# Down projections of a decoder layer on TensorE: column blocks in pairs, four of eleven inner blocks by seven products instead of eight

## The reference

```python
def swiglu(x, w_gate, w_up, w_down):
    return (jax.nn.silu(x @ w_gate) * (x @ w_up)) @ w_down
...
h = x
f = swiglu(rmsnorm(h, g_ffn1_pre[i]), w_ffn1_gate[i], w_ffn1_up[i], w_ffn1_down[i])
h = h + 0.5 * rmsnorm(f, g_ffn1_post[i])
u = rmsnorm(h, g_mix_pre[i])
...
h = h + rmsnorm(o, g_mix_post[i])
f = swiglu(rmsnorm(h, g_ffn2_pre[i]), w_ffn2_gate[i], w_ffn2_up[i], w_ffn2_down[i])
h = h + 0.5 * rmsnorm(f, g_ffn2_post[i])
```

## Time and profile before

| | |
|---|---|
| three runs | 1891.41, 1890.99, 1890.77 us; median 1890.99 |
| span of the profiled execution | 1889.1 us |
| what lies around the span, by the median | 1.9 us |
| PE, DVE, ACT, POOL busy in the span | 1878.1, 1080.5, 883.9, 112.8 us |
| matmuls | 8658 |
| DMA | 371.54 MB, mean 197 GB/s |

### The profile page before, as it was taken

How to read it: one execution, slowest core, us unless ns; L and a number is a source line. 1 busy time by engine, 2 the same in 40 slices (tenths; PEclk the granted TensorE clock), 3 DMA queues, 4 the chain that set the end, 5 groups by cost and what they waited for, 6 DMA issues and landing times.

```text
span 1889.1 us, 24728 instructions
## 1 busy us (share of the span) xinstructions
PE 1878.1 (99%) x8658; PEld 1550.4 (82%) x8658; DVE 1080.5 (57%) x1208; ACT 883.9 (47%) x1179; POOL 112.8 (6%) x162
## 2 busy tenths in 40 slices
PE   9999999999999999999999999999999999999998
PEld 7888888888888888888888888888888888888886
DVE  5555555455544446777896755555555454444565
ACT  6444444444444346555555644444444344344563
POOL 1000000000000001013551100000000000000010
PEclk9999999999999999999999999999999999999999
DMA  7666666666665655655556566666666666656554
GB/s 258 202 207 202 203 193 193 210 214 215 204 202 196 200 195 165 201 168 167 152 178 204 165 212 207 203 203 207 202 193 193 202 229 198 201 192 207 191 190 145
DMA packets 214115, 371.54 MB, mean 197 GB/s; under 512 B 16592, under 2 KB 41632, under 8 KB 213664
## 3 DMA queue, kind: packets, MB, share of 16 engines
q1 hardware_dynamic: 213040, 367.20, 61.5%
q10 hardware_dynamic: 1008, 3.46, 0.5%
HBM read 358.01 MB, written 2.10 MB: 191 GB/s over the span
## 4 chain that ended last, share of the span: by engine, by line
PE 98%; DVE 1%; ACT 0%; issue 0%; POOL 0%; POOLq 0%; DVEq 0%; ACTq 0%
PE bank L533 31%; PE bank L535 31%; PE bank L534 31%; PE bank L846 1%; PE bank L637 1%; PE bank L875 1%; PE bank L857 1%; PE bank L693 0%; PE bank L821 0%; DVE w_rest L1340 0%; DVE x_rest L1355 0%; PE bank L606 0%; PE bank L596 0%; PE bank L610 0%; PE bank L683 0%; DVE resid L1364 0%
## 5 line engine op out<-in xcount | busy, mean ns | idle before, releaser
L1340 DVE TENSOR_TENSOR w_rest<-raw,w_high 128x1024 fp32r<-128x1024 f32 x654 | 801.6, 1228 | 700.2 <-ACT w_high L988 696.6
L988 ACT CAST w_high<-raw 128x1024 fp32r<-128x1024 f32 x654 | 685.0, 1050 | 895.6 <-PE bank L535 754.3
L533 PE MATMUL bank<-w_high,x_high 128*128 128x512 f32 (+1 forms) x1912 | 745.9, 390 | 0.7 <-DVE x_rest L1695 0.2
L535 PE MATMUL bank<-w_high,x_rest 128*128 128x512 f32 (+1 forms) x1912 | 741.1, 388 | 0.0
L534 PE MATMUL bank<-w_rest,x_high 128*128 128x512 f32 (+1 forms) x1912 | 740.6, 387 | 0.0
L533 PEld LDWEIGHTS bank<-w_high,x_high 128*128 128x128 f32 x1912 | 359.1, 188 | 74.5 <-issue 1.9
L535 PEld LDWEIGHTS bank<-w_high,x_rest 128*128 128x128 f32 x1912 | 359.0, 188 | 74.3
L534 PEld LDWEIGHTS bank<-w_rest,x_high 128*128 128x128 f32 x1912 | 359.2, 188 | 71.6
L533 PE MATMUL bank<-w_high,h_high 128*128 128x512 f32 x704 | 274.2, 390 | 0.0
L535 PE MATMUL bank<-w_high,h_rest 128*128 128x512 f32 x704 | 273.9, 389 | 0.0
L534 PE MATMUL bank<-w_rest,h_high 128*128 128x512 f32 x704 | 273.9, 389 | 0.0
(11 more groups left out here) (164 smaller groups left out, 735.9 us busy)
## 6 DMA issues: line engine op xcount, KB each, us to landing
raw<-in_w_ffn_up SPq DMA_DIRECT2D x176, 512.0 KB, 4.6
raw<-in_w_ffn_down SPq DMA_DIRECT2D x176, 512.0 KB, 4.3
raw<-in_w_ffn_gate SPq DMA_DIRECT2D x174, 512.0 KB, 4.5
raw<-in_w_qkv SPq DMA_DIRECT2D x68, 512.0 KB, 3.9
raw<-in_w_o SPq DMA_DIRECT2D x32, 512.0 KB, 4.1
raw<-in_w_ple_gate SPq DMA_DIRECT2D x32, 512.0 KB, 4.2
branch<-branch SPq DMA_DIRECT2D x320, 32.0 KB, 1.9
resid<-in_x SPq DMA_DIRECT2D x8, 256.0 KB, 6.6
```

The source lines that it names most:

```text
L533: nc.tensor.matmul(o[:, 0:width], xh, wh, start=first and c == 0, stop=False)
L535: ins = nc.tensor.matmul(o[:, 0:width], xr, wh, start=False, stop=last and c == chunks - 1)
L988: nc.scalar.copy(slot(n, k)[0], raw[:, k]).then_inc(w_high_done, 1)
L1340: nc.vector.tensor_tensor(to_rest, raw[:, k], to_high.bitcast(F32), ALU.subtract).then_inc(w_rest_done, 1)
```

## The change

Column blocks are taken in pairs, 2j and 2j + 1. Of the eleven inner blocks of 512 rows (four chunks), the first four are done as groups. For such a block the product of a 2 x 2 arrangement of activations (two token halves, two chunk pairs) by a 2 x 2 arrangement of weight slots (b11, b12 in the upper two chunks, b21, b22 in the lower two; the second index is the column block) takes seven products instead of eight. Each product is 6 matmuls on one 128 x 512 output. Two use raw weight slots and one each the sums

- sum1 = b11 + b12, then sum2 = sum1 + b22, then sum4 = sum2 + b21, made one after another in place by DVE;
- sum3 = b12 + b22, made in place by POOL, when DVE's first sum has read b12.

The seven products in order are b22, b21, b11, sum1, sum3, sum2, then a plain slot, then sum4. Activations need four combinations for each group (`combine`, `combine_rest` on DVE, a rounding on ACT); they are made during the first pair and kept in `x_high` and `x_rest` for the second. The other 14 slots of each column block stay plain, 12 matmuls each. A pair has 56 positions in the hand-written order (`PAIR_ORDER`, computed in the kernel's head): 6 plain, group 0, 3 plain, group 1, 3 plain, group 2, 3 plain, group 3, 9 plain.

Each position, also that of a sum, uses one place of the four of `w_high` and `w_rest`. In the ring `raw` only plain slots, b22 and b21 have a place. b11 and b12 go to two buffers in `branch` (`chain`), loaded by SP after b22. b22 keeps its place until DVE's second sum and POOL's sum have read it, b21 until DVE's third.

Four products accumulate in banks 4 to 7 over all four groups of a pair; the other three go straight into the accumulators. ACT copies the first of the four, DVE adds them up and adds them to both blocks' accumulators (`fix_odd`, six operations, and `fix_even`, two). Squares, gains, the load of `p` and its transposes are moved to places in the new order. POOL's program has the sums between the norm factors.

```diff
+    def group(i, inner):
+        return ([(kind, None, i) for kind in ("b22", "b21", "b11", "sum1", "sum3", "sum2")] + inner
+                + [("sum4", None, i)])
...
+    PAIR_ORDER = (plains(0, G0, G0 + 6) + group(0, plains(0, G0 + 6, G0 + 7)) + plains(0, G0 + 7, G0 + 10)
+                  + group(1, plains(1, G0, G0 + 1)) + plains(1, G0 + 1, G0 + 4)
+                  + group(2, plains(1, G0 + 4, G0 + 5)) + plains(1, G0 + 5, G0 + 8)
+                  + group(3, plains(0, G0 + 10, G0 + 11)) + plains(0, G0 + 11, FS) + plains(1, G0 + 8, FS))
...
+    COMBINE_AT = [0] + [at - 7 for at in GROUP_AT[1:]]
...
 # SP
+                        if kind in RING_KINDS:
+                            free_place(j, t)
+                            k = ring_item(j, t)[1]
...
+                            sp.dma_start(raw[:, k], src).then_inc(w_landed[k], 16)
+                        if kind == "b22":
+                            for b, end in ((0, "sum4"), (1, "sum3")):
+                                if i:
+                                    sp.wait_ge(w_rest_done, n0 + PAIR_OPS * j + PLACE[end, None, i - 1] + 1)
...
+                                sp.dma_start(chain(j, b), part(2 * i, 2 * j + b)).then_inc(chain_landed[b], 16)
 # POOL
+                        pool.wait_ge(w_landed[k], 4 * (n0 - LAG * f + at) - 4 * k + 16)
+                        pool.wait_ge(sum_ready, SUMS * groups + SUM_AT["sum1"])
+                        nc.gpsimd.tensor_tensor(chain(j, 1), chain(j, 1), raw[:, k], ALU.add
+                                                ).then_inc(pool_sum_ready, 1)
 # PE
+            def group_product(n, kind, i, o, first, last):
+                pe.wait_ge(w_rest_done, n + 1)
...
+                for c in range(CPS):
...
+                    nc.tensor.matmul(o[:], xh, wh[:, c, :], start=first and c == 0, stop=False)
+                    nc.tensor.matmul(o[:], xh, wr[:, c, :], start=False, stop=False)
+                    ins = nc.tensor.matmul(o[:], xr, wh[:, c, :], start=False, stop=last and c == CPS - 1)
...
+                        if t == T_EVEN + 1:
+                            pe.wait_ge(fixed_odd, 2 * f + j + 1)
 # ACT
+            def high_down(n0, f, j, t):
...
+                elif kind == "b11":
+                    act.wait_ge(chain_landed[0], 16 * (groups + i + 1))
+                    src = chain(j, 0)
+                elif kind == "sum3":
+                    act.wait_ge(pool_sum_ready, groups + i + 1)
+                    src = chain(j, 1)
+                else:
+                    act.wait_ge(sum_ready, SUMS * (groups + i) + SUM_AT[kind])
+                    src = chain(j, 0)
+                act.wait_ge(w_used, n - RING + 1)
+                nc.scalar.copy(w_high[:, n % RING], src).then_inc(w_high_done, 1)
 # DVE
+            def rest_down(n0, f, j, t):
...
+                dve.wait_ge(w_high_done, n + 1)
+                nc.vector.tensor_tensor(w_rest[:, n % RING], src, w_high[:, n % RING].bitcast(F32), ALU.subtract
+                                        ).then_inc(w_rest_done, 1)
...
+                if kind == "b11":
+                    dve.wait_ge(chain_landed[1], 16 * (groups + i + 1))
+                    nc.vector.tensor_tensor(turns, turns, b12, ALU.add).then_inc(sum_ready, 1)
+                elif kind == "sum1":
+                    nc.vector.tensor_tensor(turns, turns, b22, ALU.add).then_inc(sum_ready, 1)
+                else:
+                    nc.vector.tensor_tensor(turns, turns, b21, ALU.add).then_inc(sum_ready, 1)
...
+                def combine(i):
+                    chunks = slice(CB * i, CB * i + CB)
+                    dve.wait_ge(moved_rest, f * MOVED + i + 1)
+                    step(nc.vector.tensor_tensor(whole, h_high[:, chunks, :].bitcast(F32),
+                                                 h_rest[:, chunks, :].bitcast(F32), ALU.add))
...
+                    nc.vector.tensor_tensor(mixed[:, 2], a21, a11, ALU.subtract)
+                    step(nc.vector.tensor_tensor(mixed[:, 0], a21, a22, ALU.subtract))
+                    step(nc.vector.tensor_tensor(mixed[:, 1], a11, mixed[:, 0], ALU.subtract))
+                    nc.vector.tensor_tensor(mixed[:, 3], a12, mixed[:, 1], ALU.subtract).then_inc(combined, 1)
...
+                        if j == 0 and t in COMBINE_AT:
+                            combine(COMBINE_AT.index(t))
+                        if j == 0 and t - 2 in COMBINE_AT:
+                            combine_rest(COMBINE_AT.index(t - 2))
+                        if t == T_FIX - 1:
+                            fix_odd(j)
```

More of the change, by code:

```diff
@@ L333, in layer_program @@
         pair_bank, o_bank, head_bank = bank[6], bank[7], bank[4:6]
+        P_FIRST, P_SUM2, P_SUM1, P_SUM3 = bank[4:8]
+        MIXED_AT = {"sum1": 0, "sum2": 1, "sum3": 2, "b22": 3}
         def o_place(q):
@@ L544, in use_slot, with use_last_slots @@
                 ins.then_inc(w_used, 1)
-            def use_last_slots(n, k, high, rest, chunk, pair, slots=2, first=False, after=None, between=None):
+            def use_last_slots(n, k, high, rest, chunk, pair, slots=2, first=False, after=None, between=None,
+                               go_on=False):
                 for t in range(T):
@@ L553, in use_last_slots @@
                         ins = products(n + m, t, k + m, high, rest, chunk + CPS * m, pair[t], first and m == 0,
[L554 removed]
+                                       m == slots - 1, between if t == T - 1 and m == slots - 1 else None, go_on)
                         if t == 0 and m == slots - 1:
@@ L771, in down @@
                 last = 2 if f else LAST_DOWN
[L772 to L783, removed]
+                even, odd = acc[b0 % 2], acc[(b0 + 1) % 2]
@@ new lines, in down @@
+                target = {"b11": P_FIRST, "b22": odd[0], "b21": even[0], "sum4": even[1],
+                          "sum1": P_SUM1, "sum2": P_SUM2, "sum3": P_SUM3}
+                for j in range(NBD // 2):
+                    pe.wait_ge(branch_ready, CREDIT - 1 + 2 * NBD * f + 2 * j)
+                    for t, (kind, which, i) in enumerate(PAIR_ORDER):
+                        n = n0 + PAIR_OPS * j + t
+                        if j == NBD // 2 - 1 and t >= PAIR_OPS - last:
+                            break
+                        if t == GROUP_AT[0]:
+                            pe.wait_ge(branch_ready, CREDIT - 1 + 2 * NBD * f + 2 * j + 1)
+                            pe.wait_ge(turn_rest, u_h + BPB)
+                        if t == T_EVEN + 1:
+                            pe.wait_ge(fixed_odd, 2 * f + j + 1)
+                        if kind == "plain":
+                            if j == 0 and i < BPB * MOVED:
+                                pe.wait_ge(moved_rest, f * MOVED + i // BPB + 1)
+                            elif j == 0:
+                                pe.wait_ge(turn_rest, u_h + i - BPB * MOVED + 1)
+                            pe.wait_ge(w_rest_done, n + 1)
+                            pair = odd if which else even
+                            for tile in range(T):
+                                ins = products(n, tile, n % RING, h_high, h_rest, CPS * i, pair[tile],
+                                               i == G0 and not (which and tile == 0),
+                                               i == FS - 1 or (which == 1 and tile == 1 and i == G0 + 7),
+                                               go_on=which == 1 and i >= G0 + 8)
+                            ins.then_inc(w_used, 1)
+                        else:
+                            if j == 0:
+                                pe.wait_ge(comb_rest, GROUPS * f + i + 1)
+                            group_product(n, kind, i, target[kind],
+                                          i == 0 and target[kind] is not even[0] and target[kind] is not even[1],
+                                          i == GROUPS - 1 and target[kind] is not even[0] and target[kind] is not even[1])
+                        if j == 0 and t == 0:
@@ L1087, in ffn @@
                     n = n0 + 2 * KS * i
-                    ahead(n, 0, KS - 1)
+                    ahead(n, 0, KS - 1, late=late)
                     silu(i)
-                    ahead(n, KS - 1, 4)
+                    ahead(n, KS - 1, 4, late=late)
                     high_moved(i)
-                    ahead(n, KS + 3, KS - 3)
+                    ahead(n, KS + 3, KS - 3, late=late)
                 last_high()
             def down(n0, b0, job, f):
[L1096 to L1119, removed]
-                        else:
[L1121 to L1126, removed]
-                    else:
-                        boundary(U_MIX, G_MIX, S_QKV, J_MIX, 0, square_last)
```

276 lines of the change are left out of this document (231 added, 45 removed).

## The result

The changed kernel takes 1924.97 us, the median of four executions (1924.76 to 1929.47), against 1891.0 before: ratio 1.0185, 95% interval 1.0171 to 1.0200. It is 34.0 us slower; 21.7 were forecast.

A forecast was written before the change was run, and what follows sets the result against it. TensorE's matmuls were taken to bound the kernel, all else hiding under them. -21.8 gain + 37.1 groups + 4.8 combinations + 1.6 loads = +21.7, giving 1912 us; range 1888 to 1936, the forecast's own 1902 to 1926.

The forecast's parts named there:

- The gain of 21.8 us: TensorE in the down projections: 6 fewer matmuls in each of 16 groups, 96 in all at 0.2267 us.
- GpSimd's sum at 2.36 us: Time of GpSimd's 128x1024 sum3, by slope from smaller adds; bounds 2.96 and the 1.01 of 384 columns.
- the mutual hold: DVE and GpSimd each wait for the other's operation to end; DVE is held to 6.2, sum1's remainder 0.67 late.
- the prediction's total by that figure: With GpSimd's sum at the skill's estimated 2.13 us, the kernel would be about 17 us slower instead of 21.
- One group on paper, 2.3 us: DVE remainders late at sum1 0.67, sum3 0.90, inner plain slot 0.75 us; 2.3 x 16 = 37.1 us.
- The combinations, +4.8: First pair's activation combinations on DVE: b11's remainder some 0.8 us later in three later groups, 3 x 2 x 0.8.
- The loads, +1.6: SP's queue after the third sum: b21's remainder 0.1 to 0.3 us late, 12 groups x 0.13.
- rival (c): Loads bind: at 1.6 us a slot +6 to +10, 1920; at 2.0, +36, 1948; chance 13%.
- The clock, costed at nothing: TensorE's clock in the down projections: stalls stay under 1.6 us, so no cost from a clock fall.

The follow-up runs named there:

- the 8-column run: Against the changed kernel, GpSimd adds only 8 of sum3's 1024 columns, the rest left out, waits unchanged: 1903.82 us, ratio 1.0066.
- the best version: Changed kernel with b21 loaded before the chain loads, sum3 on DVE, inner plain slot behind sum1 and sum3 behind sum2: 1884.20 us, ratio 0.9965.
- the version with both repairs: Changed kernel with b21 loaded ahead of the chain loads and sum3 made by DVE: 1891.67 us, ratio 1.0004.
- the ceiling: Changed kernel with b21 loaded first; groups' remainders and sums, GpSimd's sum and combinations cut to 8 columns: 1869.43 us, ratio 0.9885.

## Why the prediction was right, and where it was off

The direction, the range and the mechanism held. Point by point:

*The gain of 21.8 us.* 96 matmuls fewer on the page, and 21.7 us in the run that covers them.

*GpSimd's sum at 2.36 us and the mutual hold.* 2.39 measured; DVE's remainder beside it 2.50 us. The hold is worth 20.0 us, 1.25 a group, the largest cost that a single repair takes away. Without it (the 8-column run) the kernel was still 12.7 us slower than before, because of the loads. The Trainium skill (GPSIMD Engine Reference, section 2.1) has a floor of 2.5 cycles an element, by which, at the 1.2 GHz that the prediction took, the sum would be an estimated 2.13 us; the trace has 2.39, above that floor. (Less 0.23 us in 16 groups the prediction's total by that figure is 18.0 us and not 17.)

*One group on paper, 2.3 us.* 0.75 + 0.88 + 0.74 = 2.37 in the first group, term by term within 0.1 us. The working from one remainder to the next carried: 1.13 us between starts also for a remainder behind a sum. Without its term for the loads the forecast is 1911.1 us; with b21 first, which takes the loads' cost away, 1912.08 was measured.

*The combinations, +4.8.* 3.8 with the loads repaired, nothing in the changed kernel itself, where the late b21 covers them. Right as a price, wrong as a term of this sum. So two errors partly offset each other: the loads and the combinations together cost 16.7 us (1924.97 against 1908.30), where the forecast had 6.4. In the best version the combinations cost 8.8. That DVE has the fourth sum too, and that there is less other lateness to hide under, would explain it; no run separates the two.

*The loads, +1.6.* This is the step that failed. They cost 12.9 us, rival (c), about 1.5 of it by way of the clock. Two things were mis-sized. The rate was taken from the peak of a burst (368 GB/s). Behind the first group the windows show 298 and then 245 GB/s while b21 is waited for, and between 645 and 657 us 261 to 308 all along. Five slots took 11.4 us behind the first group and 13.2 behind the one before 662 (first issue 644.03, b21 rounded from 657.19) instead of about 10. And b21 was placed last in the queue behind two loads that are needed after it; the prediction noted the queue but went on as if arrival just before its turn were enough, with 0.8 us of slack against an uncertainty of five times 0.2 us.

*The clock, costed at nothing.* The prediction bounded single waits at 1.6 us. With b21 late they reached 3.1, and twice the clock fell, for about 1.5 us net.

The measured terms close: 1891.1 - 21.7 (gain) + 20.0 (hold) + 12.9 (loads, with the clock) makes 1902.3, and the rest, 22.7 us, is DVE's own pace in the groups and the combinations, as the version with both repairs shows by standing 22.2 us over the ceiling. What this shows is that the two repairs add up, to 0.4 us.

## What to carry to other kernels

When a change trades matmuls for operand preparation, cost it from the ring: walk one group operation by operation against when TensorE wants each operand, since DVE's idle half was of no use where six of its operations stood in a row under 4 us of matmuls. An elementwise operation given to GpSimd "for free" can hold DVE off for its full length: each 2.39 us sum cost 1.25 us here, its length less the 1.12 us that DVE would have idled. Look first for a gap in which DVE waits anyway. Order a DMA queue by when things are needed, and give a just-in-time load a margin worked out with the rate over a whole burst, not with its peak.

## What the runs showed that I had not expected

- TensorE's clock fell to 0.50 after waits inside a stream that was otherwise dense, and the length of the wait alone does not say when. By start to start, in the changed kernel it fell after waits of 3.1 us (before 665.4) and 2.5 (before 1728.7), and not after 2.15 (before 535.7). In the run without combinations it fell after 2.5 (before 536.7) and 2.1 (before 1751.4), but not after 2.65 (before 1647.7):

```profile
1647.69 0.47 PE L655 MATMUL bank<-w_high,x_high 128*128 128x512 f32 x1 [2.41 <-DVE w_rest L1558]
1648.00:1650.00 2.00, 1.34 (x7) 0.82 (x5) 2.00 (x3) 1.29 (x2) 0.00 (x0) 1.00 0.10 13
...
1751.40 0.50 PE L655 MATMUL bank<-w_high,x_high 128*128 128x512 f32 x1 [1.82 <-DVE w_rest L1558]
1752.00:1754.00 2.00, 2.00 (x6) 1.26 (x5) 2.00 (x3) 1.49 (x2) 0.00 (x0) 0.50 0.13 38
```

  In the longest fall the clock went down while TensorE still waited (664.5); in the one at 1729.5 TensorE had been at work again for 0.8 us. It was back at 1.00 after 6.1 and 4.1 us of work in the changed kernel.
- A fall can hide the next wait: behind the one at 671.5, sum1 of the following group was only 0.7 us late and not 2. That the slower matmuls gave the DMAs and DVE time to catch up is a reading of the trace, not tested by a run.
- Putting a whole 128x1024 sum on DVE cost 1.2 us in 16 groups together, against leaving it out, no more than the spread of the runs; on GpSimd the same sum cost 21 against leaving it out. Both were measured with the loads late; with b21 first no run leaves out this sum alone.
